# A two-block transformer kernel: Fourier, pooled and query/key preparation in one stage, and loads moved between stages

## The chip, the cores and the metric

One core of a Trainium2 chip runs the whole program. The metric is the device time of one execution in microseconds (us), lower is better. The engines are TensorE (PE in the profile, with PEld for its weight loads), VectorE (DVE), ScalarE (ACT), GpSimd (POOL) and SyncE (SP), which here only issues transfers.

## The reference

Two blocks work on 1024 rows of width 1024, all in fp32. The first block has two layers; besides the 1024 rows it holds 256 context rows, which the last layer doesn't update. Cut to what matters here:

```python
def fourier_mix(a, w_fourier):
    ag = a.reshape(B_, L, 4, 64).astype(jnp.float32)
    f = jnp.fft.fftn(ag, axes=(1, 3), norm='ortho').real
    return jnp.einsum('blgc,gcd->blgd', f, w_fourier)
def pool_mix(b, w_pool, pool_scale):
    pooled = windows_mean(b, (2, 4, 8, 16)) - b
    return jnp.einsum('blgc,gcd->blgd', pooled, w_pool) * pool_scale
# in each layer, p = h @ w_in
q_lat = apply_rope(rms_norm(split_heads_qk(q), qk_norm_g[0]), rope_cos, rope_sin)
k_lat = apply_rope(rms_norm(split_heads_qk(k), qk_norm_g[1]), rope_cos, rope_sin)
k_ctx = rms_norm(split_heads_qk(kc), qk_norm_g[1])
y = concat([fourier_mix(a_in), pool_mix(b_in), attention])
x = x + gate * ((y * silu(g)) @ w_out)
```

The second block projects a normed x to 14368 columns (32 of them narrow: 16 for a gate of low rank, 8 and 8 for two gates), runs two linear-attention branches and a delta-rule branch, merges the three under gates, multiplies by `w_out_2`, norms and adds to x; then follows an MLP with a squared ReLU, normed and added to x.

## The kernel before, in words

The program is a row of stages. Each stage is a block: it allocates its tiles and semaphores, and all engines wait for each other at its end. So nothing of a stage, not even a load, starts before the stage ahead has ended. Within a block each engine has its own list of instructions, written out by hand, and semaphores tie them; transfers are issued by SyncE in the order of its list.

In a layer of the first block `norm_project` writes p to HBM (`p_dram`). Then come:

- `fourier_pool(C, l, "x")`, and for the first layer also `(C, l, "c")` for the context. `ab` holds the first 512 columns of p: 256 for the Fourier branch, 256 for the pooled one. The transform over the rows is a product with a cosine and a sine table (`dft`, 2 MB for each half and kind, through two buffers), line 698, 8 groups of 8 products into `py`, taken to `yt` by ScalarE, line 734. `G` is the channel transform times `w_fourier` (line 689). The windows are products with band matrices (line 709). Lines 722 and 725 make the two branches' outputs, and VectorE copies them to `mixf` (line 749). The small tables are loaded through GpSimd's queue.
- `qk_prepare`: for each of ten tiles of 128 rows VectorE squares (line 845) and sums (847) 1024 columns of queries and keys, GpSimd makes the inverse roots (`inverse_root`, lines 55 to 59), VectorE multiplies by them (856), by the gains (861), makes the rope products (871, 875) and adds (877). TensorE turns the tile (906), ScalarE takes the queries and VectorE the keys. Tiles go in pairs: both tiles' sums, both norms, both takings.
- `attention_out`.

The second block has `load_norm_gain` (line 1281), `norm_project`, `small_projections` (the narrow columns, with loads of their own, in two groups of 16 columns, lines 1320 to 1362), `gated_linear`, `gated_delta`, `merge_out` and another `load_norm_gain`; then for each half of the rows `norm_transpose` and `mlp`; and `store_x`, one transfer of 4 MB. In `merge_out` ScalarE makes a tile's six gates (1777, 1778), GpSimd multiplies three of them by gains (1813), VectorE merges (1831 to 1840) and later scales and adds the product (1845, 1849), TensorE turns y (1866) and multiplies (1871), ScalarE takes yT (1784) and squares the product (1797).

Of the kernel before, what the change touches and what calls it, by code (L numbers as in the profile page):

```python
# [14 lines left out]
F32 = mybir.dt.float32  # L15
# [5 lines left out]
P = 128  # L21
# [175 lines left out]
def norm_transpose(C, tag, segs):  # L197
# [4 lines left out]
    with ExitStack() as st:  # L202
# [19 lines left out]
        for _, m, _ in segs:  # L222
            bases.append(n)
            n += m

# [387 lines left out]
def fourier_pool(C, l, rows):  # L613
# [4 lines left out]
    tiles, r0 = (NT, 0) if rows == "x" else (NTC, SEQ)  # L618
    length = tiles * P
    N = min(CH, length)  # L620
    NH = length // N
    tag = f"f{l}{rows}"
    with ExitStack() as st:
        sb = lambda n, s: st.enter_context(nc.sbuf_tensor(f"{tag}_{n}", s, F32))
        sem = lambda n: nc.alloc_semaphore(f"{tag}_{n}")
        ab = sb("ab", [P, tiles, 2 * FW])
        dft = sb("dft", [P, 2, tiles, N])
# [6 lines left out]
        yt = sb("yt", [P, 2, 2, length])  # L634
        pool = sb("pool", [P, 2, length])
        pg = st.enter_context(nc.psum_tensor(f"{tag}_pg", [P, 2, 2, P], F32))
        py = st.enter_context(nc.psum_tensor(f"{tag}_py", [P, 2, CH], F32))
        pp = st.enter_context(nc.psum_tensor(f"{tag}_pp", [P, 2, CH], F32))
        po = st.enter_context(nc.psum_tensor(f"{tag}_po", [P, 2, CH], F32))
# [5 lines left out]
        s_dft = [sem(f"dft_loaded{b}") for b in range(2)]  # L645
        s_g = sem("G_product")
# [3 lines left out]
        s_p = sem("pooled")  # L650
        s_pc = sem("pooled_taken")
# [3 lines left out]
        table = ins["t_dft_x" if rows == "x" else "t_dft_c"]  # L655
        order = [(h, g) for h in range(NH) for g in range(2)]

        def table_chunk(h, g):
            return table[g].rearrange("(k p) n -> p k n", p=P)[:, :, h * N:(h + 1) * N]

        @block.sync
        def _(sp):
            sp.dma_start(ab[:], C.p_dram[r0:r0 + length, 0:2 * FW].rearrange("(t p) n -> p t n", p=P)).then_inc(s_ab, 16)
            for q, (h, g) in enumerate(order):
                if q >= 2:
                    sp.wait_ge(s_y, 2 * (q - 1))
                sp.dma_start(dft[:, q % 2], table_chunk(h, g)).then_inc(s_dft[q % 2], 16)

        @block.gpsimd
        def _(pool_eng):  # L670
            pool_eng.memset(wfb[:], 0.0).then_inc(s_z, 1)
            pool_eng.memset(wpb[:], 0.0).then_inc(s_z, 1)
            pool_eng.dma_start(chan[:], ins["t_chan"].rearrange("g p n -> p g n")).then_inc(s_tab, 16)
            pool_eng.dma_start(band[:], ins["t_band"]).then_inc(s_tab, 16)
            pool_eng.dma_start(psc[:].rearrange("p a b -> p (a b)"),
                               ins["pool_scale"][l].partition_broadcast(P)).then_inc(s_tab, 16)
            pool_eng.wait_ge(s_z, 2)
            for g in range(4):
                o = QK * (g % 2)
                pool_eng.dma_start(wfb[o:o + QK, g // 2, o:o + QK], ins["w_fourier"][l, g]).then_inc(s_wd, 16)  # L680
                pool_eng.dma_start(wpb[o:o + QK, g // 2, o:o + QK], ins["w_pool"][l, g]).then_inc(s_wd, 16)

        @block.tensor
        def _(pe):
            pe.wait_ge(s_tab, 48)
            pe.wait_ge(s_wd, 16 * 8)
            for g in range(2):
                for c in range(2):
                    mm = pe.matmul(pg[:, g, c, :], chan[:, g, :], wfb[:, c, :], start=True, stop=True)
            mm.then_inc(s_g, 1)  # L690
            pe.wait_ge(s_ab, 16)
            for q, (h, g) in enumerate(order):
                pe.wait_ge(s_dft[q % 2], 16 * (q // 2 + 1))
                for c in range(2):
                    if q >= 1:
                        pe.wait_ge(s_yc, 2 * (q - 1) + c + 1)
                    for k in range(tiles):
                        mm = pe.matmul(py[:, c, 0:N], ab[:, k, c * P:(c + 1) * P], dft[:, q % 2, k, :],
                                       start=(k == 0), stop=(k == tiles - 1))
                    mm.then_inc(s_y, 1)  # L700
            for t in range(tiles):
                if t >= 2:
                    pe.wait_ge(s_pc, t - 1)
                for g in range(4):
                    near = [(t, 0 if t == 0 else 2 if t == tiles - 1 else 1)]
                    near += [(t - 1, 3)] * (t > 0) + [(t + 1, 4)] * (t < tiles - 1)
                    o = QK * (g % 2)
                    for q, (src, kind) in enumerate(near):
                        mm = pe.matmul(pp[o:o + QK, t % 2, (g // 2) * P:(g // 2 + 1) * P],
                                       ab[:, src, FW + g * QK:FW + (g + 1) * QK], band[:, kind, g, :],  # L710
                                       start=(q == 0), stop=(q == len(near) - 1))
                mm.then_inc(s_p, 1)
            pe.wait_ge(s_gc, 1)
            pe.wait_ge(s_wp, 1)
            pe.wait_ge(s_yc, 2 * len(order))
            for t in range(tiles):
                pe.wait_ge(s_pc, t + 1)
                if t >= 2:
                    pe.wait_ge(s_oc, t - 1)
                for c in range(2):  # L720
                    for g in range(2):
                        pe.matmul(po[:, t % 2, c * P:(c + 1) * P], yt[:, g, c, t * P:(t + 1) * P], G[:, g, c, :],
                                  start=(g == 0), stop=(g == 1))
                for c in range(2):
                    mm = pe.matmul(po[:, t % 2, FW + c * P:FW + (c + 1) * P], pool[:, c, t * P:(t + 1) * P],
                                   wpb[:, c, :], start=True, stop=True)
                mm.then_inc(s_o, 1)

        @block.scalar
        def _(act):  # L730
            for q, (h, g) in enumerate(order):
                for c in range(2):
                    act.wait_ge(s_y, 2 * q + c + 1)
                    act.copy(yt[:, g, c, h * N:(h + 1) * N], py[:, c, 0:N]).then_inc(s_yc, 1)

        @block.vector
        def _(dve):
            dve.wait_ge(s_tab, 48)
            dve.wait_ge(s_wd, 16 * 8)
            dve.tensor_tensor(wpb[:], wpb[:], psc[:], ALU.mult).then_inc(s_wp, 1)  # L740
            dve.wait_ge(s_g, 1)
            dve.tensor_copy(G[:], pg[:]).then_inc(s_gc, 1)
            for t in range(tiles):
                dve.wait_ge(s_p, t + 1)
                dve.tensor_copy(pool[:, :, t * P:(t + 1) * P],
                                pp[:, t % 2, 0:2 * P].rearrange("p (c n) -> p c n", c=2)).then_inc(s_pc, 1)
            for t in range(tiles):
                dve.wait_ge(s_o, t + 1)
                dve.tensor_copy(C.mixf[:, r0 // P + t, :], po[:, t % 2, :]).then_inc(s_oc, 1)


def qk_prepare(C, l):


# [2073 lines left out]
```

## Time and profile before

| | us |
|---|---|
| median of three runs | 5631.78 |
| lowest, highest | 5621.04, 5641.57 |
| the profiled execution | 5622.34 |
| its span, first to last instruction | 5620.5 |
| busy: TensorE, VectorE, ScalarE, GpSimd | 4696.4, 2425.6, 1675.9, 665.5 |
| mean granted TensorE clock | 0.923 |

The profile is that of one execution. A row of its timeline gives the start and the length in us, the engine (SPq and the like are its queue), the line of the kernel, and what is written from what; in brackets stands how long the engine had been idle and what released it. The granted clock is TensorE's as a share of 2.4 GHz; it has two levels, 1.2 and 2.4 GHz.

### The profile page before, as it was taken

How to read it: one execution, taken by the hardware profiler on the slowest of the kernel's cores; microseconds unless marked ns; L12 is line 12 of the kernel's file. 1: busy time of each engine (PE TensorE's matmuls, PEld its weight loads, DVE VectorE, ACT ScalarE, POOL GpSimd, SP SyncE). 2: the span in 40 equal slices, each digit the busy share in tenths (PEclk: the TensorE clock that was granted, in tenths of full speed). 3: DMA queues.
4: the chain of work that ended last, by engine and by line, in shares of the span. 5: the costliest groups of instructions: out<-in, count | busy, mean ns of one | idle time of the engine just before them, and what ended most of it. 6: DMA issues, size and time to landing. Idle time of an engine off the chain costs nothing. (4 is left out here: it accounts for less than half of the span.)

```text
span 5620.5 us, 60949 instructions
## 1 busy us (share of the span) xinstructions
PE 4696.4 (84%) x23497; PEld 3663.1 (65%) x23497; DVE 2425.6 (43%) x2981; ACT 1675.9 (30%) x3029; POOL 665.5 (12%) x614
## 2 busy tenths in 40 slices
PE   6997289879855988999999996987588858799798
PEld 3884156438633657888888874886477743577676
DVE  3221676431146753111111115878577746333333
ACT  2120055321103542111111114764544423222322
POOL 1000300010021001000000002456011114000000
PEclk8998599989977999999999997999799979899899
DMA  4343211143312013323223221111100035221222
GB/s 159 103 133 132 74 48 46 39 157 110 134 57 79 35 47 111 101 99 100 90 92 104 95 68 45 50 60 49 54 31 31 20 141 201 84 92 67 94 90 90
DMA packets 241333, 479.39 MB, mean 85 GB/s; under 512 B 28856, under 2 KB 64156, under 8 KB 240748
## 3 DMA queue, kind: packets, MB, share of 16 engines
q1 hardware_dynamic: 239648, 471.63, 24.4%
q0 software_dynamic: 1488, 5.11, 0.3%
q8 instruction: 126, 2.06, 0.1%
q14 instruction: 71, 0.58, 0.0%
HBM read 362.40 MB, written 114.29 MB: 85 GB/s over the span
## 5 line engine op out<-in xcount | busy, mean ns | idle before, releaser
L519 DVE TENSOR_TENSOR p_wl<-p_raw,p_wh 128x2048 fp32r<-128x2048 f32 x96 | 220.0, 2292 | 796.9 <-ACT p_wh L460 796.9
L460 ACT CAST p_wh<-p_raw 128x2048 fp32r<-128x2048 f32 x96 | 183.6, 1912 | 832.4 <-PE p_ps L370 823.2
L370 PE MATMUL p_ps<-p_wh,him 128*128 128x512 f32 x1024 | 400.8, 391 | 8.1 <-POOL lom L503 4.1
L370 PE MATMUL p_ps<-p_wh,lom 128*128 128x512 f32 x1024 | 400.0, 391 | 0.0
L370 PE MATMUL p_ps<-p_wl,him 128*128 128x512 f32 x1024 | 399.9, 391 | 0.0
L523 DVE COPY p_stg<-p_ps 128x512 f32<-128x512 f32 x168 | 115.9, 691 | 633.4 <-PE p_ps L370 610.6
L370 PE MATMUL p_ps<-p_wh,hi 128*128 128x512 f32 x896 | 353.3, 394 | 18.0 <-DVE p_wl L519 9.8
L370 PE MATMUL p_ps<-p_wl,hi 128*128 128x512 f32 x896 | 351.4, 392 | 0.0
L370 PE MATMUL p_ps<-p_wh,lo 128*128 128x512 f32 x896 | 351.2, 392 | 0.0
L370 PE MATMUL p_ps<-him,p_wh 128*128 128x512 f32 x768 | 298.8, 389 | 0.0
L370 PE MATMUL p_ps<-him,p_wl 128*128 128x512 f32 x768 | 298.8, 389 | 0.0
L370 PE MATMUL p_ps<-lom,p_wh 128*128 128x512 f32 x768 | 298.8, 389 | 0.0
L464 ACT COPY p_stg<-p_ps 128x512 f32<-128x512 f32 x168 | 98.3, 587 | 633.4 <-PE p_ps L370 604.7
L1092 PE MATMUL a_ps<-a_w,a_yT 128*128 128x512 f32 x576 | 263.5, 602 | 4.7 <-DVE a_up L1235 4.7
L2633 DVE TENSOR_TENSOR u_wl<-u_raw,u_wh 128x2048 fp32r<-128x2048 f32 x64 | 146.7, 2292 | 200.3 <-ACT u_wh L2605 200.3
L2523 PE MATMUL u_ps<-hiu,u_wh 128*128 128x512 f32 x512 | 201.1, 393 | 30.6 <-DVE u_wl L2633 30.6
L370 PEld LDWEIGHTS p_ps<-p_wh,him 128*128 128x128 f32 x1024 | 193.2, 189 | 49.3 <-DVE p_wl L519 5.1
L1676 PE MATMUL g_pa<-g_X 128*128 128x128 f32 x1344 | 176.0, 285 | 53.9 <-POOL g_X L1662 53.9
L370 PEld LDWEIGHTS p_ps<-p_wl,him 128*128 128x128 f32 x1024 | 193.3, 189 | 40.1
L370 PEld LDWEIGHTS p_ps<-p_wh,lom 128*128 128x128 f32 x1024 | 193.2, 189 | 40.1
L2523 PE MATMUL u_ps<-u_wh,u_uh 128*128 128x512 f32 x512 | 201.4, 393 | 11.1 <-DVE u_ul L2642 11.1
L1676 PEld LDWEIGHTS g_pa<-g_X 128*128 128x128 f32 x1344 | 169.9, 202 | 59.1 <-POOL g_X L1662 57.2
(401 smaller groups left out, 10043.2 us busy)
## 6 DMA issues: line engine op xcount, KB each, us to landing
p_raw<-w_in SPq DMA_DIRECT2D x96, 1024.0 KB, 5.7
pn_dram<-p_stg SPq DMA_DIRECT2D x128, 256.0 KB, 2.0
u_raw<-w_up SPq DMA_DIRECT2D x32, 1024.0 KB, 5.4
u_raw<-w_down SPq DMA_DIRECT2D x32, 1024.0 KB, 4.8
p_dram<-p_stg SPq DMA_DIRECT2D x112, 256.0 KB, 2.0
m_w<-w_mod SPq DMA_DIRECT2D x12, 2048.0 KB, 8.2
pt_dram<-p_stg SPq DMA_DIRECT2D x96, 256.0 KB, 2.0
d_raw<-pt_dram SPq DMA_DIRECT2D x24, 512.0 KB, 5.7
```

What stands on the lines that cost most here:

```text
L370: mm = pe.matmul(ps[:, u, :], lhsT, rhs, start=(kk == 0 and q == 0), stop=(kk == KD - 1 and q == 2))
L460: act.copy(wh[:, kh], raw[:, kh]).then_inc(s_wh[kh], 1)
L464: act.copy(stg[:, u % SG, :], ps[:, u, :]).then_inc(s_eA, 1)
L519: dve.tensor_tensor(wl[:, kh], raw[:, kh], wh[:, kh], ALU.subtract).then_inc(s_wl[kh], 1)
L523: dve.tensor_copy(stg[:, u % SG, :], ps[:, u, :]).then_inc(s_eD, 1)
L1092: mm = pe.matmul(po, yT[:, t % 2, k, :], w[:, k, half * CH:(half + 1) * CH], start=(k == 0), stop=(k == KD - 1))
L1676: pe.matmul(pa[:, m % 2, lev, :], X[:, b, lev, sl], X[:, b, lev, sl], start=True, stop=True)
L2523: mm = nc.tensor.matmul(ps_ap, lhs[a], rhs[b], start=(start and q == 0), stop=(stop and q == 2))
L2633: dve.tensor_tensor(wl[:, b], raw[:, b], wh[:, b], ALU.subtract).then_inc(s_wl[b], 1)
```

## The change

One stage, `prepare`, takes the place of `fourier_pool` and `qk_prepare`. Both sets of rows go through it together. On VectorE only the sums, the norms and the rope products are left; the gains are multiplied into the rope tables once (`cg`, `sg`). ScalarE squares the tiles and makes all copies out of PSUM. TensorE's turns stand between its table products. Pooled windows are kept in `mixf` itself. All loads go through SyncE's queue, in one written order. In the linear-attention branch the norm of a head's chunks is done in the steps 1 to 4 of the next head instead of 1, 3, 5 and 6. The narrow columns are loaded and split in the stage of constants (`second_constants`) and multiplied as one group of 32. `w_out_2` and the gain after the merge are loaded by the delta-rule branch's SyncE. In `merge_out` ScalarE makes the gates of tile t+2 ahead of taking yT of tile t+1, and the MLP's gain is loaded there. The MLP's first weights are loaded in `norm_transpose`, and the output rows are stored tile by tile by `mlp`. Tiles that are never alive together share a buffer, `spare`.

```diff
+def prepare(C, l):
...
+            load_qk(0)
+            sp.dma_start(ab[:], C.p_dram[0:tiles * P, 0:2 * FW].rearrange("(t p) n -> p t n", p=P)).then_inc(s_ab, 16)
+            load_dft(0)
+            load_qk(1)
+            sp.dma_start(chan[:], ins["t_chan"].rearrange("g p n -> p g n")).then_inc(s_tab, 16)
...
+            load_qk(2)
+            load_dft(1)
+            sp.dma_start(band[:], ins["t_band"]).then_inc(s_tab, 16)
...
+            load_qk(3)
+            load_qk(4)
+            load_dft(2)
+            load_qk(5)
+            load_qk(6)
+            load_dft(3)
...
+            pe.wait_ge(s_ab, 16)
+            for d in range(UX):
+                token_dft(d)
+                if d == 3:
+                    gains()
+                if d >= 1:
+                    turn(d - 1)
+            for t in range(NT):
+                windows(t)
+            turn(UX - 1)
...
+            turn(UX)
+            pe.wait_ge(s_wp, 1)
+            pe.wait_ge(s_yc, UX + UC)
+            for t in range(tiles):
+                branch_out(t)
+                if t == 3:
+                    turn(UX + 1)
...
+            squares(0)
+            squares(1)
+            for d in range(UX):
+                squares(d + 2)
+                take_dft(d)
...
+                if d >= 1:
+                    take_qk(d - 1)
...
+            for n in range(2):
+                roots(n)
+            pool.wait_ge(s_tab, 48)
+            pool.wait_ge(s_wd, 16 * 8)
+            pool.tensor_tensor(wpb[:], wpb[:], psc[:], ALU.mult).then_inc(s_wp, 1)
+            for n in range(2, NTA):
+                roots(n)
...
+            sums(0)
+            sums(1)
+            rope_tables()
+            dve.drain()
+            for n in range(NTA):
+                normed(n)
+                if n + 2 < NTA:
+                    sums(n + 2)
...
+            for h in range(2):
+                for k in range(KD):
+                    for q, (a, x) in enumerate(((C.narrow_hi, C.hi), (C.narrow_hi, C.lo), (C.narrow_lo, C.hi))):
+                        mm = pe.matmul(pl[0:2 * RANK, h, :], a[:, k, :], x[:, k, h * CH:(h + 1) * CH],
+                                       start=(k == 0 and q == 0), stop=(k == KD - 1 and q == 2))
+                mm.then_inc(s_l, 1)
...
-                if n > 0 and c in (1, 3, 5, 6):
-                    norm(n - 1, *{1: (0, 2), 3: (2, 4), 5: (4, 6), 6: (6, 8)}[c])
+                if n > 0 and 1 <= c <= 4:
+                    norm(n - 1, 2 * (c - 1), 2 * c)
...
             load(0)
-            sp.dma_start(w[:], ins["w_out_2"][0].rearrange("(k p) n -> p k n", p=P)).then_inc(s_w, 16)
             load(1)
...
             for t in range(NT):
+                if t + 2 < NT:
+                    gates(t + 2)
                 if t + 1 < NT:
                     take(t + 1)
-                if t + 2 < NT:
-                    gates(t + 2)
...
             load(0)
             sp.wait_ge(s["conv"], 1)
             load(1)
+            sp.dma_start(C.w_out[:], ins["w_out_2"][0].rearrange("(k p) n -> p k n", p=P)).then_inc(C.s_w_out, 16)
+            sp.dma_start(C.post[:], ins["ln_mix_post_2"][0].partition_broadcast(P)).then_inc(C.s_post, 16)
...
-            for kh in range(2):
-                up(0, kh)
...
+            for t in range(TT):
+                sp.wait_ge(s_x, t + 1)
+                n = TT * half + t
+                sp.dma_start(out[0, n * P:(n + 1) * P, :], C.x_sb[:, n, :]).then_inc(C.s_out, 16)
+            if half == 1:
+                sp.wait_ge(C.s_out, 16 * NT)
...
-            load_norm_gain(C, "lg1", ins["ln_mlp_pre_2"][0])
...
-                    norm_transpose(C, f"n3{half}", [(NT // 2 * half, NT // 2, 0)])
-                    mlp(C, half)
-        store_x(C, out)
+                    norm_transpose(C, f"n3{half}", [(NT // 2 * half, NT // 2, 0)], first_weights(C, half))
+                    mlp(C, half, out)
```

Where the instructions go is seen at two places. TensorE in the first layer, from its first product behind the projections; `f0x_py`, `f0x_pp` and `f0x_po` are the transform, the windows and the outputs. Before, and with the turns in a stage of their own far behind:

```order
L689 MATMUL f0x_pg<-f0x_wfb,f0x_chan 128x128 x4
L698 MATMUL f0x_py<-f0x_dft,f0x_ab 128x512 x64
L709 MATMUL f0x_pp<-f0x_band,f0x_ab 64x128 x88
L722 MATMUL f0x_po<-f0x_G,f0x_yt 128x128 x4
L725 MATMUL f0x_po<-f0x_wpb,f0x_pool 128x128 x2
```

Now (`f_nrm` is a normed tile of queries and keys, x8 its turn):

```order
L749 MATMUL f_ps<-f_dft,f_ab 128x512 x16
L739 MATMUL f_ps<-ident,f_nrm 128x128 x8
L749 MATMUL f_ps<-f_dft,f_ab 128x512 x8
L739 MATMUL f_ps<-ident,f_nrm 128x128 x8
L749 MATMUL f_ps<-f_dft,f_ab 128x512 x8
L792 MATMUL f_ps<-f_wfb,f_chan 128x128 x4
L739 MATMUL f_ps<-ident,f_nrm 128x128 x8
L749 MATMUL f_ps<-f_dft,f_ab 128x512 x8
```

A turn now stands behind every group of eight table products but the first, and the gain product comes in the middle.

ScalarE in the merge, in a steady step, before (`y_g` and `y_mg` are a tile's two kinds of gates, `y_yT` the turned rows, `y_junk` the square of the product):

```order
L1797 ACTIVATE y_junk,y_ms<-y_po 128x1024
L1784 COPY y_yT<-y_pt 128x1024
L1777 ACTIVATE y_g<-y_g 128x1024
L1778 ACTIVATE y_mg<-y_mg 128x1024
L1777 ACTIVATE y_g<-y_g 128x1024
L1778 ACTIVATE y_mg<-y_mg 128x1024
```

Now:

```order
L1816 ACTIVATE y_g<-y_g 128x1024
L1817 ACTIVATE y_mg<-y_mg 128x1024
L1816 ACTIVATE y_g<-y_g 128x1024
L1817 ACTIVATE y_mg<-y_mg 128x1024
L1823 COPY y_yT<-y_pt 128x1024
L1836 ACTIVATE y_junk,y_ms<-y_po 128x1024
```

The copy of yT, which waits for TensorE's turn, moved from ahead of the six gate operations to behind them.

## Rows read from the trace of the kernel before

**Rows 1.** SyncE's timeline, edges of the fused part: start us, us, what.

```profile
445.57 0.40 SPq L663 DMA_DIRECT2D f0x_ab<-p_dram  x1
...
688.48 0.38 SPq L1011 DMA_DIRECT2D v<-p_dram  x1
...
1517.13 0.39 SPq L663 DMA_DIRECT2D f1x_ab<-p_dram  x1
...
1730.07 0.38 SPq L1011 DMA_DIRECT2D v<-p_dram  x1
```

**Rows 2.** Windows view, queries' and keys' stage (us; busy of each engine; clock; DMA).

```profile
568.00:688.00 120.00, 19.69 (x80) 15.69 (x80) 85.99 (x109) 5.74 (x10) 48.00 (x30) 0.51 0.16 49
```

**Rows 3.** Timeline of the first layer's Fourier stage.

```profile
465.00 58.00 PE L698 MATMUL f0x_py<-f0x_dft,f0x_ab 128*128 128x512 f32 x128 [2.51 <-DMA f0x_dft<-t_dft_x]
...
474.97 0.58 ACT L734 COPY f0x_yt<-f0x_py 128x512 f32<-128x512 f32 x1 [34.74 <-PE f0x_py L698]
...
481.83 0.58 ACT L734 COPY f0x_yt<-f0x_py 128x512 f32<-128x512 f32 x1 [6.28 <-PE f0x_py L698]
...
522.93 10.10 PE L709 MATMUL f0x_pp<-f0x_band,f0x_ab 128*64 128x128 f32 x176
...
535.94 0.69 DVE L749 COPY mixf<-f0x_po 128x512 f32<-128x512 f32 x1 [0.65 <-PE f0x_po L725]
```

**Rows 4.** Timeline of the queries' and keys' stage: VectorE, then GpSimd.

```profile
582.67 1.23 DVE L856 TENSOR_TENSOR q_nrm<-q_raw,q_rs 128x1024 f32<-128x1024 f32 x1 [2.37 <-POOL q_rs L59]
...
583.97 1.31 DVE L861 TENSOR_TENSOR q_nrm<-q_nrm,q_gq 128x512 f32<-128x512 f32 x2
...
589.51 1.22 DVE L856 TENSOR_TENSOR q_nrm<-q_raw,q_rs 128x1024 f32<-128x1024 f32 x1
...
579.23 2.94 POOL L57 TENSOR_TENSOR q_rs<-q_rs,minus_half 128x16 f32<-128x16 f32 x1 [0.16 <-issue]
```

**Rows 5.** Timeline of TensorE: a turn in that stage, one in the merge.

```profile
589.65 1.97 PE L906 MATMUL q_pt<-ident,q_nrm 128*128 128x128 f32 x8 [22.25 <-DVE q_nrm L877]
...
4681.35 1.09 PE L1866 MATMUL y_pt<-ident,y_y 128*128 128x128 f32 x8 [3.88 <-DVE y_y L1840]
```

**Rows 6.** Windows view where the queue is full: Fourier stage, merge.

```profile
446.00:456.00 10.00, 0.00 (x0) 0.00 (x0) 0.00 (x0) 0.00 (x0) 6.32 (x12) 0.54 0.98 341
...
4608.00:4618.00 10.00, 1.97 (x8) 1.57 (x8) 7.43 (x5) 0.00 (x0) 1.53 (x1) 0.50 1.03 409
```

**Rows 7.** Timeline of the narrow projections' stage.

```profile
3360.26 0.40 SPq L1320 DMA_DIRECT2D s_w<-w_in  x1
...
3389.14 2.28 DVE L1356 COPY s_low<-s_pl 16x2048 f32<-16x2048 f32 x1 [24.11 <-PE s_pl L1337]
...
3406.55 0.36 SPq L1453 DMA_DIRECT2D g_z<-pt_dram  x1
```

**Rows 8.** Timeline of the merge: GpSimd, then VectorE.

```profile
4685.53 7.97 POOL L1813 TENSOR_TENSOR y_g<-y_g,y_on 128x1024 f32<-128x1024 f32 x3 [9.20 <-ACT y_mg L1778]
...
4681.21 1.28 DVE L1845 SCALAR_TENSOR_TENSOR y_mo<-y_po,y_ms,y_post 128x1024 f32<-128x1024 f32 x1
...
4687.93 3.36 DVE L1831 SCALAR_TENSOR_TENSOR y_g<-y_mg,y_g 128x1024 f32<-128x1024 f32 x1 [4.12 <-POOL y_g L1813]
...
4701.97 1.28 DVE L1845 SCALAR_TENSOR_TENSOR y_mo<-y_po,y_ms,y_post 128x1024 f32<-128x1024 f32 x1
```

**Rows 9.** Timeline of SyncE and TensorE at small stages.

```profile
2100.16 0.38 SPq L1281 DMA_DIRECT2D scale<-ln_mix_pre  x1
...
2102.95 0.80 SPq L565 DMA_DIRECT2D p_xt<-x_dram  x2
...
5226.57 0.93 SPq L2504 DMA_DIRECT2D u_raw<-w_up  x2
...
5236.28 0.79 PE L2523 MATMUL u_ps<-hiu,u_wh 128*128 128x512 f32 x1 [15.10 <-DVE u_wl L2633]
...
5608.44 0.39 SPq L2805 DMA_DIRECT2D out<-x_sb  x1
```

More of the change, by code:

```diff
@@ L654, in fourier_pool, with cols @@
         block = st.enter_context(nc.Block())
[L655 to L659, printed above, removed]
+        order = [(h, g) for h in range(2) for g in range(2)]
+        UX, UC = 8, 0 if last else 4
+        def cols(n):
+            return (512, 1024) if n >= NT and last else (0, 1024)
         @block.sync
@@ L662, in _, with load_qk, load_dft @@
         def _(sp):
[L663 to L664 removed]
+            def load_qk(n):
+                if n >= NR:
+                    sp.wait_ge(s_free, n - NR + 1)
+                a, z = cols(n)
+                sp.dma_start(raw[:, n % NR, a:z], C.p_dram[n * P:(n + 1) * P, Q0 + a:Q0 + z]).then_inc(s_raw[n % NR], 16)
+            def load_dft(q):
+                h, g = order[q]
@@ L683, in _ @@
+            load_qk(5)
+            load_qk(6)
+            load_dft(3)
+            for n in range(7, NTA):
+                load_qk(n)
         @block.tensor
         def _(pe):
[L685 to L700, printed above, removed]
@@ L711, in _, with branch_out @@
                                        start=(q == 0), stop=(q == len(near) - 1))
                 mm.then_inc(s_p, 1)
[L713 to L718, printed above, removed]
+            def branch_out(t):
+                if t < 2:
+                    pe.wait_ge(s_pc, tiles)
+                else:
                     pe.wait_ge(s_oc, t - 1)
@@ new lines, in _ @@
+            for t in range(NT):
+                windows(t)
+            turn(UX - 1)
+            if not last:
+                pe.wait_ge(s_dftc, 32)
+                for d in range(UC):
+                    context_dft(d)
+                for t in range(NT, NTA):
+                    windows(t)
+            turn(UX)
[5 more added lines that the diff above has]
+                    turn(UX + 1)
@@ L729, in _, with squares @@
         @block.scalar
         def _(act):
[L731 to L734, printed above, removed]
+            def squares(n):
+                a, z = cols(n)
+                act.wait_ge(s_raw[n % NR], 16 * (n // NR + 1))
+                if n >= 2:
+                    act.wait_ge(s_ms, n - 1)
+                act.activation(sq[:, n % 2, a:z], raw[:, n % NR, a:z], ACT.Square).then_inc(s_sq, 1)
@@ new lines, in _, with roots @@
+            for t in range(NT):
+                take_windows(t)
+            take_qk(UX - 1)
+            for d in range(UC):
+                take_context_dft(d)
+            for t in range(NT, tiles):
+                take_windows(t)
+            take_qk(UX)
+            for t in range(tiles):
+                take_out(t)
+                if t == 3:
+                    take_qk(UX + 1)
+        @block.gpsimd
+        def _(pool):
+            pool.memset(wfb[:], 0.0).then_inc(s_z, 1)
+            pool.memset(wpb[:], 0.0).then_inc(s_z, 1)
+            def roots(n):
+                a, z = cols(n)
+                pool.wait_ge(s_ms, n + 1)
+                inverse_root(C, pool, rs[:, n % 2, a // QK:z // QK], ss[:, n % 2, a // QK:z // QK], QK).then_inc(s_rs, 1)
+            for n in range(2):
[5 more added lines that the diff above has]
+                roots(n)
```

539 lines of the change are left out of this document (255 added, 284 removed).

## The prediction

> **What bounds the kernel now.** I read four views, in this order. The queue of SyncE in order of time first, because every stage opens with its loads: it gives the stages' edges. The part that the change fuses lasts from 445.57 to 688.48 us in the first layer, 242.9 us, and from 1517.13 to 1730.07 us in the second, 212.9 us [rows 1]. It is 8% of the span of 5620.5 us, and its stages follow each other with nothing shared. Then busy time by window: in the queries' and keys' stage VectorE is busy for 86.0 of 120 us and TensorE for 19.7, at a granted clock of 0.51 [rows 2]. The timeline of the Fourier stage shows the reverse: TensorE runs for 58 us without a break from 465.00 while VectorE does nothing [rows 3]. So one half is bound by TensorE, the other by VectorE's chain with GpSimd, and each could lie under the other. Last, the timelines of the small stages show engines waiting for a load that opens the stage [rows 7, 9].
>
> **The fused stage, first layer.** Its length is the loads, then TensorE's list.
> - Loads: the first product needs one tile of queries and keys (0.52 MB), `ab` of ten tiles (2.62 MB) and a table chunk (2.10 MB), 5.24 MB. Before, 19.4 us passed from the first issue to the first product, at 341 GB/s [rows 1, 3, 6]; 4.19 MB of that was needed, the rest was GpSimd's tables (1.5 MB) and 0.7 MB of the next chunk. With the same 0.7 MB ahead, 5.94 MB take 17.5 us and I add 1: start at 18.5. Bounds: 15.4 (5.24 MB alone) and 25 (the 14 small loads get in between).
> - Token products: the first group took 9.97 us (the clock was at its lower level, after idling), the others 6.87 each [rows 3]: 9.97 + 7 x 6.87 = 58.1.
> - Turns: ten of 8 transposes. They took 1.97 us each at the lower clock and 1.09 where TensorE had just worked [rows 5]. In the fused list they stand between products, so I take 1.1: 11. Bound above: 20.
> - Windows 10.1 for eight tiles and 2 for the two of the context (one neighbour less), the context product 3.6 (a sixteenth of the columns that took 58), the gain product 1, ten branch outputs at 1.34, from copy to copy [rows 3], 13.4. First waits and the last copy: 1.5.
> - Sum: 18.5 + 58.1 + 11 + 12.1 + 3.6 + 1 + 13.4 + 1.5 = 119.2; I add 1.8 for handshakes: **121, 122 less than before**.
>
> What must stay hidden: VectorE's work for one tile took 6.84 us, from 582.67 to 589.51, of which the two gain multiplications and their hand-over 1.5 [rows 4]. The gains now go into the rope tables once (3 us), squares go to ScalarE, one reduction of the same length as the norm product (1.2) stays: 6.84 - 1.5 + 1.2 = 6.5 us a tile. TensorE's step in that part is 6.87 + 1.1 = 8.0. VectorE starts late: the rope tables come behind about 6.8 MB, at 25; tables 28, tile 0 ready at 33.5, and TensorE asks for it at 18.5 + 16.8 = 35.3. GpSimd, whose power operation takes 2.94 us of some 4.6 for a tile's roots [rows 4], first waits for `band` and `pool_scale`, behind 10.7 MB in the queue (34), so that tile 2 is ready at 48 and wanted at 52. After that the lead grows by 1.5 us a tile. ScalarE has a square of twice the elements of a copy (about 1.1) and three copies of 0.58 [rows 3] for each step of 8.0: hidden. If that cover fails, each late tile lengthens the stage by its lateness.
>
> On SyncE's queue the table chunks now stand behind tiles' loads that wait for VectorE. `load_dft(2)` stands behind tile 4, free at about 36, and is wanted at 53; `load_dft(3)` behind tile 6, free at about 50, wanted at 68. 2.1 MB take 8 us: hidden.
>
> **Second layer.** 4.72 MB, start at 17; no context product and windows (-5.6), eight outputs (-2.7), two half turns (-1.1), so 121 - 1.5 - 9.4 = 110.1: **103 less**.
>
> **Narrow projections.** From 3360.26 to 3406.55 us, 46.3 us [rows 7]. The loads and the split (4.8 us, what is left of 28.9 ahead of the 24.1 of the products) move to the constants' stage; 96 products, some of them at the lower clock, become 48 at 0.23 to 0.25, 11.5; the copy of 2.28 becomes two, one of them under products, 0.7 left; eight logit products with their copies fill most of the last 15 us, 1.7 each, and run now through a ring of four with two engines, about 0.9 each, 7; transposes and edges 2. Sum 21.2: **25 less** (18 to 28, by whether the logit products stay at 1.7). The constants' stage, 2.8 us until the next issue [rows 9], gets longer by four issues and the split: **+2** (0 to 5).
>
> **Merge.** The weights are 4.19 MB that stood between tile 0 and tile 1. The queue moved 409 GB/s there [rows 6]: 10.2 us. By the Trainium skill ("DMA: Bandwidth & Descriptors", Specifications) HBM gives a core about 358 GB/s; with that the load would be worth 11.7. The row decides. They now load in the delta-rule branch, whose queue is nearly empty.
> The other edit is the order on ScalarE: the gates of tile t+2 ahead of the taking of yT. A period is 20.8 us (4681.21 to 4701.97), of which VectorE idles 4.12, waiting for GpSimd's first gain product, and while GpSimd's three (7.97 us) run, an operation of 1.23 stretches to 3.36 [rows 8] and the next one alike. With gates early the idle goes, but the third gain product now meets VectorE as well: 20.8 - 4.1 + 2.1 = 18.7. Six such periods give 12.6. By the Trainium skill ("SBUF — State Buffer", the rule on the shared port pair) a VectorE operation with two SBUF inputs and a GpSimd operation that reads SBUF exclude each other fully; nine such operations, one other and three gain products in a row make 19.5, a gain of 8 instead of 12.6. The first tiles, whose gates waited for the queue and then for the taking, give some 7 more (0 to 14). Sum: **30 less**, bounds 10 and 42.
>
> **Small stages.** The gain load with a stage of its own before the MLP goes; its like before the projections took 2.8 us [rows 9], of which an edge's 0.2 stays: **-2.6**. The MLP's first weights are issued at 5226.57 and its first product starts at 5236.28 [rows 9]; of these 9.7 us the transfer now lies under the normalising. Two casts of 2048 columns and their hand-overs stay, about 4.5. Twice 5.2: **-10.4**. The output leaves at 5608.44 as one transfer of 4 MB and the span ends 12.1 us later [rows 9]; now three quarters of it goes tile by tile and the last 0.5 MB takes about 3: **-9** (7 to 10).
> The norm schedule in the linear-attention branch moves ScalarE's work within a head and removes none: 0. Unseen, so bounded by one norm pair (some 1.1 us) for each of 11 heads either way: -8 to +12. Weight loads beside the delta rule: 0, up to +5.
>
> **Sum.** -122 - 103 - 25 + 2 - 30 - 2.6 - 10.4 - 9 = -300. The profiled execution took 5622.3 us (span 5620.5): 5322. The runs' median, 5631.8, lies 9.4 above that execution, within the runs' spread of 21, so I move up by 3: **5325 us**. A difference under 0.3% (17 us) can't be told from no change.
>
> **Rivals.**
> 1. *The cover leaks* in the fused stage: turns at 1.97 us, the start at 25, tiles late by GpSimd's wait for `band`. For it: the lists of all five engines are coupled in one block, and GpSimd stands behind two loads. Against: 1.5 us of spare in each step. Price 9 + 6 + 10 in a layer, 50 in all: 5375.
> 2. *Merge gains the weights alone*, since VectorE and GpSimd exclude each other: -10 instead of -30: 5345.
> 3. *VectorE becomes the bound of the fused stage and the kernel gets slower.* Place: the operations on `nrm`, two SBUF inputs each, beside GpSimd's roots, as in merge [rows 8]. All seven of a tile stretched by 2.1 us make 21 us a tile and stages of 28 + 8 x 21 + 15 = 211 each, a total of 5516. To lose against before, both stages together would have to reach 456 + 74 = 530 us, from which a tile would need 28 us. In the old stage such stretching isn't there, though GpSimd worked beside VectorE: 1.23 throughout [rows 4].
> 4. *The branches gain more*: transposes and start at their lower bounds, merge at its upper: 5300.
> That the stage doesn't overlap at all is excluded by TensorE's order, which has turns between products.
>
> **Chances.** Forecast 0.60; rival 1: 0.17; rival 2: 0.12; rival 4: 0.09; rival 3, slower: 0.01; no change (an unseen cost of 300 us): 0.01. Bounds of the single terms give about 35 us to either side of 5325; rival 1 reaches 5375. Range 5290 to 5385. Faster 0.98, same 0.01, slower 0.01.
>
> **What would show it.** The stage's first and last issue on SyncE about 121 and 110 us apart. TensorE's turns near 1.1 us with a granted clock near 1 from the second product on, and idle under 5 us between products. First product at 18 to 19 us. The narrow stage near 21 us with the logit copies 0.9 apart. Merge periods of 18.7 us with three stretched VectorE operations. First MLP product 4 to 5 us after the stage's start; span end about 3 us after the last store's issue. The prediction is wrong if TensorE waits for `nrm` in most steps, if the clock falls to its lower level between the products, or if another branch lengthens by over 20 us.

## The result, and the profile after

The changed kernel takes **5342.27 us**, the median of four runs (5338.86 to 5347.66), beside 5632.65 for the kernel before: a ratio of 0.9487, 95% interval 0.947 to 0.9503. The prediction was 5325 in a range of 5290 to 5385: the sign and the size are right, and the time came out 17 us above the forecast. The profiled execution took 5340.35 us (span 5338.5), 282 less than the one before; the sum had 300.

SyncE's timeline of the changed kernel (start us, us, what) gives the stages' edges, as [rows 1, 9] did:

```profile
447.85 0.35 SPq L693 DMA_DIRECT2D f_raw<-p_dram  x1
...
561.85 0.38 SPq L1048 DMA_DIRECT2D v<-p_dram  x1
...
1387.32 0.34 SPq L693 DMA_DIRECT2D f_raw<-p_dram  x1
...
1490.91 0.38 SPq L1048 DMA_DIRECT2D v<-p_dram  x1
...
1860.35 0.39 SPq L1321 DMA_DIRECT2D scale<-ln_mix_pre  x1
...
1865.94 0.83 SPq L569 DMA_DIRECT2D p_xt<-x_dram  x2
...
3183.71 0.35 SPq L1493 DMA_DIRECT2D g_z<-pt_dram  x1
...
3742.25 0.35 SPq L1994 DMA_DIRECT2D d_causal<-t_causal  x1
...
4353.84 0.35 SPq L1798 DMA_DIRECT2D y_on<-hgrn_onorm  x1
...
4536.97 0.95 SPq L2501 DMA_DIRECT2D spare<-w_up  x2
...
4561.01 0.34 SPq L2560 DMA_DIRECT2D post<-ln_mlp_post  x1
...
5327.29 7.82 SPq L2573 DMA_DIRECT2D out<-x_sb  x4
```

With the same edges before, one line for each part (us, after minus before):

| part | predicted | measured |
|---|---|---|
| fused stage, first layer (114.0 now) | -122 | -128.9 |
| fused stage, second layer (103.6 now) | -103 | -109.3 |
| second block's projection, first load to last product | 0 | +35.8 |
| narrow projections, last product of the projection to the next stage (49.9, now 28.3) | -25 | -21.6 |
| constants' stage (5.6 now) | +2 | +2.8 |
| merge with its small stage (210.1, now 183.1) | -32.6 | -27.0 |
| MLP and output | -19.4 | -21.9 |
| linear-attention branch (558.5 now) | 0 | -8.0 |
| all the rest | 0 | -3.8 |
| sum | -300 | -282 |

So without the projection the terms together came out 18 us better than predicted (both fused stages, the MLP and the linear-attention branch better, the narrow projections, the merge and the constants worse), and one line that stood at nothing in the sum took 36 us back. The projection is the same code on the same shapes. The windows view of its steady part, before and then after (us; busy and count of PE, PEld, DVE, ACT, POOL; granted clock; DMA share, GB/s):

```profile
2500.00:2750.00 250.00, 250.00 (x1104) 207.08 (x1104) 42.04 (x36) 37.05 (x36) 0.00 (x0) 1.00 0.29 97
```

```profile
2500.00:2750.00 250.00, 250.00 (x1073) 201.23 (x1072) 41.14 (x34) 34.63 (x35) 0.00 (x0) 1.00 0.28 94
```

The clock is granted in full in both and TensorE never idles, yet it starts 1073 products where it started 1104: one every 0.2330 us instead of 0.2264. Over the projection's 5376 products that is 35.5 us. It is some 7 ns in each product, and the profile shows no wait between them.

TensorE's timeline of the fused stage, first layer:

```profile
464.57 16.42 PE L749 MATMUL f_ps<-f_dft,f_ab 128*128 128x512 f32 x32 [19.98 <-DMA f_dft<-t_dft_x]
480.83 1.04 PE L739 MATMUL f_ps<-ident,f_nrm 128*128 128x128 f32 x8
481.70 7.03 PE L749 MATMUL f_ps<-f_dft,f_ab 128*128 128x512 f32 x16
488.57 1.04 PE L739 MATMUL f_ps<-ident,f_nrm 128*128 128x128 f32 x8
...
529.14 10.10 PE L769 MATMUL f_ps<-f_band,f_ab 128*64 128x128 f32 x176
...
551.89 1.04 PE L739 MATMUL f_ps<-ident,f_nrm 128*128 128x128 f32 x8
```

No turn shows a wait for VectorE. The first product starts 16.7 us behind the stage's first issue, the product behind a turn starts 0.87 us after the turn does, the granted clock is 1.00 from 481 us on. The merge, VectorE and then GpSimd:

```profile
4417.49 2.62 DVE L1888 TENSOR_TENSOR x_sb<-x_sb,y_mo 128x1024 f32<-128x1024 f32 x1
4420.04 3.37 DVE L1870 SCALAR_TENSOR_TENSOR y_g<-y_mg,y_g 128x1024 f32<-128x1024 f32 x1
4423.48 3.21 DVE L1875 TENSOR_TENSOR y_y<-y_g,y_o 128x1024 f32<-128x1024 f32 x1
4426.61 1.21 DVE L1870 SCALAR_TENSOR_TENSOR y_g<-y_mg,y_g 128x1024 f32<-128x1024 f32 x1
...
4437.63 2.02 DVE L1888 TENSOR_TENSOR x_sb<-x_sb,y_mo 128x1024 f32<-128x1024 f32 x1
```

```profile
4416.66 8.95 POOL L1852 TENSOR_TENSOR y_g<-y_g,y_on 128x1024 f32<-128x1024 f32 x3 [0.58 <-ACT y_mg L1817]
```

VectorE no longer idles there. Its last operation of a tile (line 1888) starts at 4417.49, 4437.63, 4457.16, 4471.30, 4492.79, 4507.27, 4520.84 and 4534.57: periods of 20.1, 19.5, 14.1, 21.5, 14.5, 13.6 and 13.7 us. VectorE has a tile to merge in the first five of them only. Its operations of 1.23 us that lasted 2.0 to 3.4 instead number 4, 4, 1, 5 and 1 in those five; GpSimd's gain products come in rows of three, from 4416.66, 4432.90, 4449.16, 4469.85 and 4484.79 on, 8.9 us each row.

### The profile page after: what moved, and what is told of

Read it like the earlier page. It is cut to its first block and busy times, and to the rows that moved or that the text cites. A ratio compares the mean times of both kernels' runs of the same rounds, so it can differ in the third digit from the quotient of the medians.

```text
span 5338.5 us, 60419 instructions
## 1 busy us (share of the span) xinstructions
PE 4679.9 (88%) x23441; PEld 3635.5 (68%) x23441; DVE 2344.3 (44%) x2876; ACT 1725.8 (32%) x3111; POOL 643.3 (12%) x580
## 5 line engine op out<-in xcount | busy, mean ns | idle before, releaser
L2690 DVE TENSOR_TENSOR u_wl<-spare,u_wh 128x2048 fp32r<-128x2048 f32 x64 | 146.5, 2292 | 189.4 <-ACT u_wh L2662 189.4
L1716 PE MATMUL g_pa<-g_X 128*128 128x128 f32 x1344 | 176.5, 286 | 49.1 <-POOL g_X L1702 49.1
L2580 PE MATMUL u_ps<-hiu,u_wh 128*128 128x512 f32 x512 | 201.0, 392 | 19.6 <-DVE u_wl L2690 19.6
```

Of the source, the lines that this page charges most:

```text
L1716: pe.matmul(pa[:, m % 2, lev, :], X[:, b, lev, sl], X[:, b, lev, sl], start=True, stop=True)
L2580: mm = nc.tensor.matmul(ps_ap, lhs[a], rhs[b], start=(start and q == 0), stop=(stop and q == 2))
L2690: dve.tensor_tensor(wl[:, b], raw[:, b], wh[:, b], ALU.subtract).then_inc(s_wl[b], 1)
```

## The experiments

Stage lengths below are from SyncE's timeline, edges as above. Kernels that leave a stage alone serve as repeats of it: the merge took 178.3 to 183.4 us in eight executions with its changed code, the linear-attention branch 558.5 to 565.4 in eleven, the projection with the narrow part 1317.7 to 1320.0 in seven.

**Where the tiles start.** The change puts new tiles between the activations `him`, `lom` and the projection's weight tiles. The last, `bg`, has 16 bytes in a partition and takes up 32. The tiles follow each other in a partition, so their distances can be worked out from their sizes: from `him` to the high part of the weights, `p_wh`, 81920 bytes before and 87072 now; `lom`, `him`, `p_wh` and `p_wl` stand multiples of 4096 apart otherwise.

`aligned`, weight tiles back on a multiple of 128:

```diff
-                C.bg = sb("bg", [P, B_HEADS], F32, s3)
+                C.bg = sb("bg", [P, 32], F32, s3)[:, 0:B_HEADS]
```

> The changed kernel with the tile bg made 128 bytes wide instead of 16, so that the three weight tiles of the second block's projection start at a multiple of 128 bytes again, as in the kernel before (now they start 32 bytes off, while the activations him and lom start on a multiple). Theory A, addresses: TensorE's products of 512 columns come one every 0.2265 us while both operands have the same remainder, and one every 0.233 us (measured in the changed kernel's projection, 1073 in 250 us instead of 1104) when they differ; then the projection, from its first load to its last product, takes 1254 us as before instead of 1290, and the time is 5342 - 36 = 5306. Theory B, the program (another place of the code, more tiles resident, other loads under way): the interval stays at 0.233 and the time at 5342.

`before_shifted`, the kernel before with one tile more:

```diff
                 C.lo = s3.enter_context(nc.sbuf_tensor("lom", [P, KD, SEQ], F32R))
+                s3.enter_context(nc.sbuf_tensor("shim", [P, 8], F32))
```

> The kernel before with a tile of 32 bytes put between lom and the projection's tiles, nothing else. Theory A: the interval between products goes from 0.2265 to 0.233 us, the projection from 1254 to 1290 us, the time to 5633 + 36 = 5669. Theory B: 5633, unchanged.

`both_off`, `bg` allocated ahead of `him`:

```diff
+                C.bg = sb("bg", [P, B_HEADS], F32, s3)
                 C.hi = s3.enter_context(nc.sbuf_tensor("him", [P, KD, SEQ], F32R))
...
-                C.bg = sb("bg", [P, B_HEADS], F32, s3)
```

> The changed kernel with bg placed ahead of him and lom: all operands of the projection start 32 bytes off a multiple of 64. Theory A in its first form, that only the difference between the two operands counts (as the first block's projection suggests, whose operands are both 32 off and whose products come every 0.226 us): interval 0.2265, time about 5306. In its second form, that the streamed or the loaded operand has to start on a multiple of 64: 0.233, 5342. Theory B: 5342.

Measured: `aligned` 5341.47 us (ratio 0.9478, 0.9465 to 0.949), interval unchanged at 0.233: the theory in the form that it had there, equal remainders of both operands at 128 bytes, failed, and with it that expectation. `before_shifted` 5667.0 (ratio 1.0057, 1.0042 to 1.0072): the old kernel gets slower by 32 bytes, 1073 products in 250 us. `both_off` 5315.24, projection with narrow part 1282.4 us instead of 1317.8:

```profile
2250.00:2500.00 250.00, 250.00 (x1105) 207.13 (x1104) 40.44 (x33) 35.38 (x34) 0.00 (x0) 1.00 0.28 93
```

In `both_off` the weights start where they start in the changed kernel, and in `before_shifted` the activations start where they did before; so neither operand's own place decides, nor does the program. Equal remainders at 64 or 128 bytes are not enough either (`aligned`). All cases sort by the distance between the two operands. Two more kernels, `bg` made 256 and 512 bytes wide, and the first of them again, in five executions:

```diff
-                C.bg = sb("bg", [P, B_HEADS], F32, s3)
+                C.bg = sb("bg", [P, 64], F32, s3)[:, 0:B_HEADS]
```

> The changed kernel with bg made 256 bytes wide. What the three runs so far say together: products came every 0.2265 us where the projection's weight tile starts a multiple of 512 bytes behind the activations (before: 81920, both_off: 87040, the first block's projection: 98304, the MLP: 32768), and every 0.233 us where it starts 32 or 128 bytes beyond such a multiple (changed kernel, before_shifted, aligned). Here the distance is 87296, 256 beyond a multiple of 512. Theory A with a period of 256 bytes or less: 0.2265 us, time about 5308. With a period of 512: 0.233 us, about 5342. Theory B, no rule of distances: either, without a pattern.

> The changed kernel with bg made 512 bytes wide: a distance of 87552 bytes, a multiple of 512 and not of 1024. Theory A with a period of 512 or less: 0.2265 us, time about 5308. With a period of 1024: 0.233 us, 5342.

> The kernel of apart_256 once more, now timed against the kernel before, since its 5306.9 us was one execution and the term that it measures is the one that the prediction did not have. Theory A: 5304 to 5311 us, a ratio of 0.942 to 0.943, 31 to 38 us under the changed kernel's median of 5342. Rival: much of the difference was the spread from run to run (the changed kernel's four runs lie within 9 us); then the median is above 5325.

| kernel | `him` to `p_wh`, bytes | over a multiple of 512 | products in 250 us | time |
|---|---|---|---|---|
| before | 81920 | 0 | 1104 | 5632.65 |
| before_shifted | 81952 | 32 | 1073 | 5667.0 |
| changed | 87072 | 32 | 1073 | 5342.27 |
| aligned | 87168 | 128 | 1073 | 5341.47 |
| both_off | 87040 | 0 | 1105 | 5315.24 |
| apart_256 | 87296 | 256 | 1105 | 5306.86 |
| apart_512 | 87552 | 0 | 1105 | 5307.69 |

The times of `both_off`, `apart_256` and `apart_512` are of one execution each.

The same window of `aligned`, of `before_shifted` and of `apart_256`:

```profile
2500.00:2750.00 250.00, 250.00 (x1073) 201.15 (x1072) 40.97 (x34) 34.53 (x34) 0.00 (x0) 1.00 0.28 93
```

```profile
2500.00:2750.00 250.00, 250.00 (x1073) 201.14 (x1072) 39.77 (x33) 34.66 (x32) 0.00 (x0) 1.00 0.27 90
```

```profile
2500.00:2750.00 250.00, 250.00 (x1105) 207.01 (x1104) 41.13 (x34) 33.99 (x33) 0.00 (x0) 1.00 0.29 96
```

`apart_256_timed` gives 5308.43 us (5306.39 to 5313.73), ratio 0.9423, interval 0.941 to 0.9437. Theory A stands with a period of 256 bytes or less (a divisor of 256 that is above 128, so 256, if the pattern is a period at all), theory B is out. Why the distance between TensorE's two operands matters isn't settled: no run here shows the memory's inside, only products of 512 columns in this projection were varied, and of the remainders only 0, 32, 128 and 256 bytes. The Trainium skill ("SBUF — State Buffer", Who interferes with whom) gives TensorE two independent read ports, one for each operand of a product, and says that it never waits on anyone. By that, place would not matter; these runs show that it does, by 0.0066 us a product.

**How well the queries and keys are hidden.** `short_products` leaves out seven eighths of each token sum:

```diff
-                for k in range(NT):
+                for k in range(1):
```

> The changed kernel with each token product of the fused stage cut to one matmul of eight, so that most of the sum over tokens is left out. Theory 1, that TensorE sets the stage and queries and keys are well hidden: the stage falls to what the queries' and keys' chain needs, at VectorE's some 7 us a tile about 10 x 7 + 20 = 90 us with the rest, so by 20 to 25 us a layer from 114 and 104. Rival, that queries and keys already nearly set the pace: the stage falls by under 8 us.

Measured: first layer 108.8 us instead of 114.0, second 96.0 instead of 103.6. The theory that TensorE alone sets the stage is wrong, the rival right. TensorE's timeline of that kernel:

```profile
500.54 1.97 PE L739 MATMUL f_ps<-ident,f_nrm 128*128 128x128 f32 x8 [2.73 <-DVE f_nrm L941]
502.30 1.91 PE L749 MATMUL f_ps<-f_dft,f_ab 128*128 128x512 f32 x2
506.94 1.97 PE L739 MATMUL f_ps<-ident,f_nrm 128*128 128x128 f32 x8 [2.73 <-DVE f_nrm L941]
```

Tiles now come every 6.4 us, VectorE's pace, which the prediction had at 6.5; VectorE begins with its first normed tile only 26.7 us after the stage's start. So VectorE's chain, with its late start, is the next bound, 5 to 8 us under TensorE's: shortening TensorE's part alone gains little more than that. (With its waits TensorE fell to a granted clock of 0.66 from 481 to 529 us; the windows behind it took 11.29 us instead of 10.10, so that the bound itself lies some 1 us lower.)

**The merge's two edits.** One undone in each kernel:

```diff
-                if t + 2 < NT:
-                    gates(t + 2)
                 if t + 1 < NT:
                     take(t + 1)
+                if t + 2 < NT:
+                    gates(t + 2)
```

> The changed kernel with ScalarE's work of the merge in the old order again: the copy of the turned tile t+1 ahead of the gates of tile t+2. The prediction's step has it that the order is worth 20.8 - 18.7 = 2.1 us a period, of which 0.9 was measured as gained (20.8 to 19.9): theory O expects the period back at 20.8, with VectorE idle 4 to 5 us of each, and the stage 5 to 13 us longer. Rival: VectorE is busy without a gap now, so the weights' early load gave everything and the order nothing: period 19.9, stage within 2 us.

For `merge_loads_back` the two transfers go from the delta-rule branch's list to the merge's, the weights behind `load(0)` and the gains behind `load(1)`:

```diff
             load(0)
+            sp.dma_start(C.w_out[:], ins["w_out_2"][0].rearrange("(k p) n -> p k n", p=P)).then_inc(C.s_w_out, 16)
             load(1)
+            sp.dma_start(C.post[:], ins["ln_mix_post_2"][0].partition_broadcast(P)).then_inc(C.s_post, 16)
```

> The changed kernel with the merge's output weights and its row of gains loaded in the merge again, between the loads of the first two tiles, and no longer in the delta-rule branch; ScalarE's new order stays. The prediction's term: 4 MB at 409 GB/s, 10.2 us longer (merge 178 to 183 becomes 188 to 193). After merge_old_order, where the old order alone brought back 21 to 25 of the some 25 us, theory W expects at most 3 to 5 us.

Measured: with the old order the merge takes 203.9 us (time 5368.04), with the loads back 184.0. (The latter's time, 5361.01, lies 19 us above the changed kernel's median, but between the two profiles only 0.8 of it is in the merge; 6.9 are in the linear-attention branch, 4.5 between the two fused stages and 4.3 in the second attention, which the edit doesn't touch.) The order is worth 20 to 26 us, the weights 1 to 6: the prediction's 10.2 is out. With the loads back VectorE's last operation of the first tile starts 72.2 us behind the stage's first issue instead of 63.7, so the transfer does cost 8.5 us there. Of these the next five periods, at 17.0 on average where the changed kernel has 18.0, make up 4.8, and the sixth, at 10.7 for 13.6, another 2.9: the later tiles meet GpSimd's products differently. VectorE's timeline with the old order:

```profile
4448.22 1.22 DVE L1888 TENSOR_TENSOR x_sb<-x_sb,y_mo 128x1024 f32<-128x1024 f32 x1
4454.44 3.36 DVE L1870 SCALAR_TENSOR_TENSOR y_g<-y_mg,y_g 128x1024 f32<-128x1024 f32 x1 [5.00 <-POOL y_g L1852]
...
4469.84 1.23 DVE L1888 TENSOR_TENSOR x_sb<-x_sb,y_mo 128x1024 f32<-128x1024 f32 x1
```

The idling of 5.0 is back in every period, as in [rows 8]. The first five periods are 21.5 on average, in the changed kernel 18.0: a gain of 3.5 each where my expectation, which went by the changed kernel's two first periods, had 0.9 (and 5 to 13 us for the stage, which took 20.8 more). The first tile is 3 us later too.

`merge_no_gains` cuts GpSimd's three gain products to one column a head (the output norm's gain is left out):

```diff
-                    pool.tensor_tensor(m, m, on[j][:].unsqueeze(1).to_broadcast([P, H, D // H]), ALU.mult).then_inc(s_gg, 1)
+                    pool.tensor_scalar(m[:, :, 0:1], m[:, :, 0:1], 1.0, None, ALU.mult).then_inc(s_gg, 1)
```

> The changed kernel with GpSimd's three gain products a tile in the merge cut to one column a head: the output norm's gain is left out of the merge. Theory L, that VectorE's operations with two SBUF inputs are stretched from 1.23 to 2.0-3.4 us only by GpSimd's products beside them: no stretched operation is left, the merge's period falls from 19.9 us (measured in the changed kernel) to what TensorE needs, 14.9 + 1.5 = 16.4, the stage by 6 x 3.5 + the first tiles' 5 to 8 = some 27 us. Rival M, that the stretches come from loads or from TensorE's traffic: they stay and the period is 19 to 20.

Measured: merge 156.7 us, period 14.6, each VectorE operation at 1.22 to 1.28, and TensorE without a gap:

```profile
4401.60 1.04 PE L1905 MATMUL y_pt<-ident,y_y 128*128 128x128 f32 x8
4402.47 13.90 PE L1910 MATMUL y_po<-spare,y_yT 128*128 128x512 f32 x32
4416.21 1.04 PE L1905 MATMUL y_pt<-ident,y_y 128*128 128x128 f32 x8
```

Theory L holds: with GpSimd's products gone no stretched operation is left in the merge. The stage fell by 26.4 us, as expected; the period fell further than the expected 16.4.

**The norms' places.** Edit: in the linear-attention branch `if n > 0 and c in (1, 3, 5, 6)` with the old pairs, instead of `1 <= c <= 4`.

> The changed kernel with the linear-attention branch's norms in the old places (beside chunks 1, 3, 5 and 6 instead of 1 to 4). Theory: the places account for the branch's 558.5 to 565.0 us in the changed kernel and its relatives instead of 566.6 and 566.8 in the two with the old places; then it is at 566 to 567 again. Rival, that it is the branch's stores and addresses or chance: within 558 to 565.

Measured: 572.3 us, above both expectations. TensorE's wait for GpSimd at its products with `g_X` adds up to 57.9 us in that run and 49.1 in the changed kernel, 8.8 of the 13.8 us between them. The three executions with the old places (566.6, 566.8, 572.3) lie above all eleven with the new ones (middle 561), but two of the three are kernels that differ in much else, and the third is one execution. So the sign is likely; the size, 6 to 11 us, is not settled.

**A version that beats both.** `early_and_gains` is `both_off` with two edits that follow from the above. In the fused stage the first `ab` and `dft` are loaded in halves with the first product's second half waiting on its own semaphore, the rope tables are loaded once and both gain variants made from them, small tables come later, and GpSimd makes five tiles' roots instead of two ahead of its wait for them. In the merge:

```diff
-                    pool.tensor_tensor(m, m, on[j][:].unsqueeze(1).to_broadcast([P, H, D // H]), ALU.mult).then_inc(s_gg, 1)
...
+                    m = g[:, b, j].rearrange("p (h n) -> p h n", h=br[j][0])
+                    dve.tensor_tensor(m, m, on[j][:].unsqueeze(1).to_broadcast([P, br[j][0], D // br[j][0]]), ALU.mult)
+                    dve.drain()
                     dve.scalar_tensor_tensor(g[:, b, j], mg[:, b, j], 1.0, g[:, b, j], ALU.add, ALU.mult)
```

> A version made from both_off (5315) with two more edits. In the fused stage the first tiles are loaded in halves, the turning tables once and ahead of what is needed later: the first product should start some 8 us behind the stage's first load and not 16.7, and VectorE's first normed tile at 18 to 20 us and not 25; theory S, that both sides are held by their start (short_products: the stage falls by only 5.2 us when seven eighths of the token products are gone), expects each stage 7 us shorter, 114 to 107 and 103 to 96. Its rival, that only one side moves or the products then wait for loads: under 3 us a layer. In the merge the three gain products a tile go from GpSimd to VectorE: theory L, that GpSimd's products cost VectorE more by stretching its operations than their own 1.3 us each, expects VectorE's period at 12.5 + 3.9 = 16.4 us instead of 19.9 and the merge 21 us shorter, at about 160; its rival, that the added work simply comes on top, expects 19.9 + 3.9 = 23.8 and the merge at 205. Together by S and L: 5315 - 14 - 21 = 5280.

Measured: **5289.21 us** (5285.13 to 5292.94), ratio 0.9389, interval 0.9375 to 0.9402. The merge takes 163.8 us, 14.5 to 19.6 less, at periods of 16.3 to 16.7: VectorE does 24 operations more and is done earlier.

```profile
4372.62 1.23 DVE L1890 TENSOR_TENSOR x_sb<-x_sb,y_mo 128x1024 f32<-128x1024 f32 x1
4373.76 1.22 DVE L1870 TENSOR_TENSOR y_g<-y_g,y_on 128x1024 f32<-128x1024 f32 x1
4375.06 1.23 DVE L1872 SCALAR_TENSOR_TENSOR y_g<-y_mg,y_g 128x1024 f32<-128x1024 f32 x1
4376.36 1.23 DVE L1877 TENSOR_TENSOR y_y<-y_g,y_o 128x1024 f32<-128x1024 f32 x1
...
4388.94 1.22 DVE L1890 TENSOR_TENSOR x_sb<-x_sb,y_mo 128x1024 f32<-128x1024 f32 x1
```

Theory S got half of its 7 us a layer: from their first issue the fused stages take 110.5 and 99.1 us instead of 114 and 102.5 to 103.6. TensorE starts 8.6 us behind the first issue, as wanted, and loses more than half of the 8.1 us again: 1.0 waiting for the second half's load, 1.1 for VectorE's first tile, 2.1 at the fourth group. TensorE, then ScalarE:

```profile
458.13 5.68 PE L760 MATMUL f_ps<-f_dft,f_ab 128*128 128x512 f32 x8 [11.90 <-DMA f_dft<-t_dft_x]
...
487.44 7.13 PE L760 MATMUL f_ps<-f_dft,f_ab 128*128 128x512 f32 x16 [2.06 <-ACT f_yt L848]
```

```profile
485.86 1.06 ACT L837 ACTIVATE f_sq<-f_raw 128x1024 f32<-128x1024 f32 x1 [8.60 <-DMA f_raw<-p_dram]
486.82 0.57 ACT L848 COPY f_yt<-f_ps 128x512 f32<-128x512 f32 x1
```

The copy that frees TensorE's bank stands on ScalarE's list behind the square of a tile whose load has not landed. That order is the changed kernel's too; there the load came in time.

## Why the prediction was right or wrong

- **Fused stage**, -225 predicted, -238 measured: the mechanism is the predicted one. The start was at 16.7 us, not 18.5. By then 5.9 MB had moved (352 GB/s over 16.7 us), as the term had it; the rate was mis-sized, for once the transfers flowed they moved 385 GB/s (449.5 to 464.5 us), and the window of [rows 6] with its 341 opens 0.4 us behind the first issue (before, it is 364 from 448 to 464 us). The handshakes (1.8) were not there, of the 1.5 for first waits and the last copy 0.9 was, and a turn adds 0.87, not 1.1. The token products took 57.5 from start to start, against 58.1.
- **Cover**: VectorE's 6.5 us a tile was 6.4, and from 481 to 529 us only one operation of 1.23 was stretched, to 1.59, though GpSimd was busy with roots for 36.7 of these 48 us; so rivals 1 and 3 fell. The spare of 1.5 us a step is right, but the prediction didn't draw from it that VectorE's chain is the next bound.
- **Narrow projections**, -25 predicted, -21.6 measured: the step "eight logit products ... about 0.9 each" failed for the second four. The copies of the first four are 0.87 apart, those of the rest 1.7:

```profile
3172.93 0.69 ACT L1390 ACTIVATE spare<-s_pg,bg 128x512 f32<-128x512 f32 x1 [19.34 <-PE s_pg L1377]
...
3177.38 0.69 ACT L1390 ACTIVATE spare<-s_pg,bg 128x512 f32<-128x512 f32 x1 [2.04 <-PE s_pg L1377]
...
3180.80 0.69 ACT L1390 ACTIVATE spare<-s_pg,bg 128x512 f32<-128x512 f32 x1 [2.73 <-PE s_pg L1377]
```

  The windows view there (columns as above):

```profile
3172.00:3175.00 3.00, 3.00 (x8) 1.29 (x8) 1.31 (x2) 1.04 (x2) 0.00 (x0) 1.00 0.00 0
3177.00:3183.00 6.00, 5.46 (x7) 1.67 (x5) 1.25 (x2) 1.37 (x2) 0.00 (x0) 0.50 0.00 0
```

  The granted clock is 1.00 up to 3176 us and 0.50 from 3177 on. Before, it was 0.50 from 3393 on, where the logits stood 1.7 apart. TensorE has no gap between these products in either kernel, so the spacing was the lower clock's; the term had put it down to the copies, which a ring of four and a second engine would have cured.
- **The projection's products**: the step that failed most is one that isn't in the sum. I took code that the diff doesn't touch to cost what it cost. Its operands moved, and the 35.5 us are more than the whole of the miss: with the distance mended the same changes give 5308, 17 us *below* the forecast. The prediction had named a branch that lengthens by over 20 us as a sign of being wrong, and here a stage did, by 35.8. That the total still came within 17 us owes something to luck: an error of 36 one way and of 18 the other.
- **Merge**, -30 predicted for its two edits, about -24 measured (-27.0 with the small stage's 2.6): the sum of two terms that were both wrong. "The weights, 10.2 us" was 1 to 6: the first tile is 8.5 us earlier, but VectorE's list of the following tiles sets the end. "The order, 18.7 for 20.8" was 18.0 for 21.5, in five periods and not six, and 3 us at the first tile. I had every period meet three stretched operations; that is the average of the five (4, 4, 1, 5 and 1), but not one of them has it, and they range from 14.1 to 21.5 us, since GpSimd's rows of three products and VectorE's periods don't keep step. The rule that I weighed there (the Trainium skill, "SBUF — State Buffer", shared port pair: the two engines exclude each other) would have given 19.5 a period. As a mechanism it describes the rows nearly: from 4416.66 to 4426.69 GpSimd has 3 products, of 2.34 each where VectorE idles beside them (at 4366.02), and VectorE 3 operations of 1.23, 10.7 us of work in 10.0. Under full exclusion no work would run side by side; here 0.7 us of it did. Rival 2, the weights alone, has it the wrong way round.
- **Small stages**: the MLP's first product starts 4.4 us after the stage's edge (predicted 4 to 5), its parts and the output gave 21.9 for 19.4; from the last stores' row the span ends at 5338.5, 3.4 us after it.
- **Norm schedule**, 0 predicted within -8 to +12, measured -8.0; `norm_old` makes the sign likely.
- The chances: the forecast's case came in, with rival 2's time (5345) reached by another way.

## What to carry to other kernels

When a change adds, drops or resizes a tile, look at every stage that allocates behind it: compare the number of products in equal windows at an equal clock, and keep the distance between TensorE's two operands a multiple of 256 bytes, as in every fast case here. When two engines block each other, price an operation by what it stretches beside it: an operation moved onto the busier engine can still win. Undo the edits of a bundle one at a time, since a right sum (merge) can hide two wrong terms.

## What the runs showed of the hardware that I had not expected

- Products of 128x512 on fp32r operands come every 0.2264 us when the operands' distance is a multiple of 256 bytes and every 0.2330 when it is 32 or 128 over, at a granted clock of 1.00, in seven kernels; 2.9% of the projection, 0.6% of the program. A common shift of all operands by 32 bytes costs nothing.
- GpSimd's products of 128x1024 stretch VectorE's of 1.23 us to between 2.0 and 3.4; its power operations of 128x16, 3.1 us long in the fused stage, hardly do (one of 1.59 from 481 to 529 us, the others of 128x1024 at 1.21 to 1.23). Width and kind of operation differ there, and I varied neither by itself.
- The granted clock fell while TensorE was busy: four products of 16 rows by 512 columns came 0.87 us apart from 3171.78 us on, then eight transposes of 32 columns, then four more such products 1.7 apart, without a gap between them; the clock was 1.00 until 3176 and 0.50 from 3177 on. In the kernel before the same eight products ran at 0.52 on average, 0.50 from the second one on.
